# A layer with 32 streamed experts: another order of the output product, an earlier refill of its buffers, and a shorter chain to the first gathered tokens

## The chip, the cores and the metric

One core of a Trainium2 chip runs the whole program. The metric is the device time of one execution in microseconds (us), and the median of some runs of the same program counts.

## The reference

One layer over 256 tokens of width 1024, all float32. A mixer (short convolutions for one half of the channels, a gated linear recurrence for the other) is followed by an output product, a residual sum and a layer norm. Then each token chooses 4 of 32 experts, and the experts' outputs are mixed by their gates and normed again.

```python
mixed = _mixer(x, ...)                       # ends in einsum('bsc,cd->bsd', mix, w_out)
x = _layer_norm(DEEPNORM_ALPHA * x + mixed, ln1_g, ln1_b)
logits = x @ w_router + b_router
top_v, top_e = lax.top_k(logits, 4);  gates = softmax(top_v)
# for every expert e, for the tokens that chose it:
h = xb @ w_gu[e] + b_gu[e]                   # 1024 -> 2048
act = min(h_glu, 7) * sigmoid(1.702 * h_glu) * (clip(h_lin, -7, 7) + 1)
y = act @ w_dn[e] + b_dn[e]                  # 1024 -> 1024
x = _layer_norm(DEEPNORM_ALPHA * x + sum_of_gated_y, ln2_g, ln2_b)
```

The weights of one expert are 8 MB (gate and up) and 4 MB (down), so that the 32 experts make 403 MB of the 421 MB that the program moves.

## The kernel before

**Buffers.** `gu_buf` holds two experts' gate/up weights, 8 rows of 1 MB each (a row is 8 KB in each of 128 partitions); they are loaded in chunks of two rows, 2 MB (`load_gu`, `stream_gu`, lines 228 and 286). `dn_buf` holds one expert's down weights, 8 rows of 512 KB, loaded in halves of four rows, 2 MB (`load_dn`, `stream_dn_chunk`, lines 231 and 291). All loads are issued by the SP queue in the order in which its block is written out (lines 226 to 328). Each waits until the TensorE has used what stood in the place: `gu_used[c]`, `dn_used[c]`, or in the loading phase a named semaphore. While the mixer runs, second-set rows 2 to 5 of `gu_buf` hold the output weights `w_out_v` (8 rows of 512 KB, two in each row of `gu_buf`), and `dn_buf` holds scratch. Expert 1's first four down rows therefore go to free places elsewhere (`dn_extra`: the two rows of `late`, half of `mix`, half of `turned`; `load_extra`, line 261), and its last four into `dn_buf` once expert 0 has used them.

**The stretch around the change.** The output product (`mixer_out`, line 886) sums 8 blocks k for 4 tiles (two token halves h, two column halves c). Its first 4 blocks (the recurrence's) go for all tiles; then each tile in turn gets its last 4 blocks and is given to VectorE (`out_ps`). VectorE adds the residual, gathers statistics, centres and scales (`residual`, `centre`, `scale`; lines 599, 589, 593); TensorE transposes the un-normed sum (line 900) and multiplies by the router (`route_part`, 927; `route_sum`, 933). `choose` (632) takes the top four, TensorE counts ranks (945 to 949), and VectorE makes from them `places` (664), a token's slot in its expert. The first block of 32 token rows is gathered by `gather_first` in three sets of four products: first half with the finished values, second half with the bias `late[:,1]` and again with a scaled selector. VectorE transposes the rows (671), and `expert_block` starts: bias rows (999), 64 gate/up products (1005), the next block's gather (955), `combine`, and 64 down products (1038). Each product is recorded as two matmuls, so 1005 has 64 records for a block.

**Block 0 and after.** `expert_block(0, ..., first=True)` is unrolled. It is followed by a branch over a loop for further blocks of expert 0 (line 1057), and by `expert(1, ...)`, which loads two loop bounds (1047 and 1048) and loops over `expert_block`. The number of blocks up to each expert stands in `bounds`; VectorE writes it (685) after block 0's rows have been transposed. SP reads it for every expert (line 280) before it can wait for the right count. VectorE's own loop starts after the gates and the remaining `places` are known: it writes `gated` (717) and the next `onehot` (709), on which TensorE's next gather waits.

Of the kernel before, what the change touches and what calls it, by code (L numbers as in the profile page):

```python
# [27 lines left out]
P = 128  # L28
SLOTS = 32
# [13 lines left out]
def trunk(nc, x, w_in, conv_w, lru_conv_w, lru_conv_b, w_rgate, b_rgate, w_igate, b_igate, lru_lambda, w_out,  # L43
# [23 lines left out]
    with ExitStack() as ctx:  # L67
# [58 lines left out]
        hot_scaled = gated[:, 1, 0:SLOTS]  # L126
# [27 lines left out]
        quiet = rows_t[:, 0:P // SLOTS, :].rearrange("p k s -> p (k s)")  # L154
        ident_v = ident[:].rearrange("p (j e) -> p j e", j=GROUPS)
# [20 lines left out]
        def like(v, tile):  # L176
# [5 lines left out]
            "x_in0", "x_in1", "params_in", "matrices_in", "router_in", "wout_in0", "wout_in1", "ln1_in", "ln2_in", "bgu_in", "bdn_in", "extra_in", "stored",  # L182
# [5 lines left out]
            "mix_lru", "mix_conv", "lru_out_ps", "out_ps",  # L188

            "wsum_in", "wsum_ps", "wr_ok", "v_ok", "var_ok", "centred", "rstd_ok", "x1_ok", "vt_ps", "vt_sb", "lpart_ps", "lpart_sb", "logits_ps", "top_ok", "exp_in", "exp_ok",  # L190
# [35 lines left out]
        def _(sp):  # L226
# [41 lines left out]
            load_gu(1, 1, 1)  # L268
            sp.wait_ge(S["out_ps"], 2 * TH)
# [59 lines left out]
        def _(pool):  # L329
# [27 lines left out]
            nc.gpsimd.memset(closed, 0.0).then_inc(S["closed_zero"], 1)  # L357
            nc.gpsimd.memset(small[:, 380:382], -0.5).then_inc(S["consts"], 1)
# [3 lines left out]
            nc.gpsimd.memset(ones_row[:], 1.0).then_inc(S["ones_row"], 1)  # L362
# [14 lines left out]
        def _(act):  # L377
# [54 lines left out]
            for h in range(TH):  # L432
                for n in (2 * h, 2 * h + 1):
                    act.wait_ge(S["vt_ps"], n + 1)
                    nc.scalar.copy(x1t[:, h, CT * (n % 2):CT * (n % 2 + 1), :],
                                   ps[:, 4 + n, :].rearrange("p (k t) -> p k t", k=CT)).then_inc(S["vt_sb"], 1)
                act.wait_ge(S["lpart_ps"], h + 1)
                nc.scalar.copy(glu[:, P * h:P * (h + 1)], ps[:, HB + h, 0:P]).then_inc(S["lpart_sb"], 1)
            act.wait_ge(S["exp_in"], 1)
# [26 lines left out]
        def _(dve):  # L466
# [136 lines left out]
            def scale_0(c):  # L603
                dve.wait_ge(S["centred"], c + 1)
                dve.wait_ge(S["rstd_ok"], 1)
                dve.wait_ge(S["vt_ps"], c + 1)
                scale(0, c, mixed(0, c), xs[:, 0, 512 * c:512 * c + 512], late[:, 1, :], S["x1_ok"])

            def centre_in_place(c):
                dve.wait_ge(S["vt_ps"], 2 + c + 1)  # L610
                v = xs[:, 1, 512 * c:512 * c + 512]
                centre(1, c, v, v, late[:, 0, :], S["centred"])

            def scale_in_place(c):
                dve.wait_ge(S["centred"], 2 + c + 1)
                v = xs[:, 1, 512 * c:512 * c + 512]
                scale(1, c, v, v, late[:, 1, :], S["x1_ok"])
# [9 lines left out]
            total = small[:, 368:370]  # L627

# [17 lines left out]
            for c in range(2):  # L646
                centre(0, c, xs[:, 0, 512 * c:512 * c + 512], mixed(0, c), late[:, 0, :], S["centred"])
# [166 lines left out]
        def _(pe):  # L814
# [87 lines left out]
            for h in range(TH):  # L902
# [259 lines left out]
```

## Time and profile before

| | before |
|---|---|
| median of 3 runs | 1021.49 us (1020.88 to 1023.22) |
| the profiled execution | 1020.78 us |
| its span, first to last instruction | 1019.0 us |
| TensorE matmul / weight load | 824.2 us (81%) / 355.9 us (35%) |
| VectorE / ScalarE / GpSimd | 246.4 / 79.5 / 7.2 us |
| DMA | 421.69 MB, mean 414 GB/s |
| chain of waits, by engine | DMA 56%, PE 36%, DVE 5%, issue 2% |

The page cuts the span into 40 slices of 25.5 us. What to read first is the line of bytes moved per slice: it is level over nearly the whole span, and lower in the first five slices and the last.

### The profile page before, as it was taken

To read this page: it belongs to the slowest core of one execution; us is meant where nothing else is said; L and a number is where in the kernel's file an instruction comes from. 1 tells how busy PE (TensorE), PEld (TensorE's weight loads), DVE (VectorE), ACT (ScalarE), POOL (GpSimd) and SP (SyncE) were. 2 spreads that over 40 slices of the span, in tenths; PEclk is the share of its full clock that TensorE was granted. 3 is DMA by queue.
4 is the path that set the end of the run, shared out by engine and by line. 5 is a ranking of instruction groups with operands and counts; after the bars stand their busy time and mean duration, and the time that the engine had idled before them with its cause. 6 is when DMAs were issued, how large, how long until landed. Compare 5 with 4: busy or idle time off the path is not lost.

```text
span 1019.0 us, 20186 instructions
## 1 busy us (share of the span) xinstructions
PE 824.2 (81%) x8447; PEld 355.9 (35%) x8448; DVE 246.4 (24%) x692; ACT 79.5 (8%) x184; POOL 7.2 (1%) x25
## 2 busy tenths in 40 slices
PE   9999879898659999985699976666865885965995
PEld 7884433333213334331133421221321332311432
DVE  2473711221112222221112211111111221210233
ACT  1040100000000000000000000000000000000010
POOL 1000000000000000000000000000000000000000
PEclk9999989999899999998799998888989799988989
DMA  9988699999999999999999999999999999999996
GB/s 327 408 355 346 266 425 425 428 428 428 428 429 428 429 428 429 428 429 429 428 429 429 428 428 429 428 429 428 428 430 428 429 429 428 429 428 428 428 428 291
DMA packets 38903, 421.69 MB, mean 414 GB/s; under 512 B 5907, under 2 KB 6347, under 8 KB 14309
## 3 DMA queue, kind: packets, MB, share of 16 engines
q1 hardware_dynamic: 36436, 420.89, 98.0%
q10 hardware_dynamic: 2400, 0.44, 0.2%
q8 instruction: 14, 0.23, 0.1%
q0 software_dynamic: 48, 0.09, 0.0%
q14 instruction: 5, 0.03, 0.0%
HBM read 420.27 MB, written 1.18 MB: 414 GB/s over the span
## 4 chain that ended last, share of the span: by engine, by line
DMA 56%; PE 36%; DVE 5%; issue 2%; SPq 0%; DVEq 0%; POOLq 0%; ACT 0%; POOL 0%
DMA dn_buf<-in_w_down_dram 56%; PE ps L1038 12%; PE ps L1005 12%; PE ps L838 5%; PE ps L886 3%; PE ps L999 2%; PE ps L857 1%; DVE act_t L730 1%; DVE lin L725 1%; DVE lin L728 1%; DVE glu L722 1%; DVE lin L723 1%; DMA gu_buf<-in_w_in_dram 1%; PE ps L918 0%; PE ps L873 0%
## 5 line engine op out<-in xcount | busy, mean ns | idle before, releaser
L1005 PE MATMUL ps<-gu_buf,rows_t 128*32 128x512 f32 x2880 | 363.8, 651 | 102.0 <-DMA gu_buf<-in_w_gate_up_dram 102.0
L1005 PEld LDWEIGHTS ps<-gu_buf,rows_t 128*32 128x32 f32 x2880 | 93.8, 115 | 362.6 <-issue 196.0
L1038 PE MATMUL ps<-dn_buf,act_t 128*32 128x256 f32 x2848 | 171.1, 385 | 52.1 <-DMA dn_buf<-in_w_down_dram 44.1
L722 DVE TENSOR_SCALAR glu<-ps 128x256 f32<-128x256 f32 x45 | 19.1, 425 | 605.2 <-PE ps L1005 605.2
L1038 PEld LDWEIGHTS ps<-dn_buf,act_t 128*32 128x32 f32 x2848 | 87.7, 110 | 123.4 <-DMA dn_buf<-in_w_down_dram 59.2
L999 PE MATMUL ps<-turned,bias_sel 128*32 128x512 f32 x360 | 50.2, 630 | 22.6 <-issue 22.6
L449 ACT ACTIVATE sig<-glu 128x256 f32<-128x256 f32 x45 | 18.8, 417 | 529.1 <-DVE glu L722 529.1
L838 PE MATMUL ps<-turned,gu_buf 128*128 128x256 f32 x256 | 55.7, 379 | 0.0
L979 PE MATMUL ps<-mix,back 32*128 32x256 f32 x720 | 52.2, 404 | 0.5 <-ACT mix L453 0.5
L955 PE MATMUL ps<-xs,onehot 128*32 128x256 f32 x736 | 50.5, 394 | 1.5 <-DVE onehot L709 1.5
L838 PEld LDWEIGHTS ps<-turned,gu_buf 128*128 128x128 f32 x256 | 48.6, 190 | 6.9 <-issue 0.4
L979 PEld LDWEIGHTS ps<-mix,back 32*128 32x128 f32 x720 | 33.0, 187 | 21.0 <-issue 18.9
L955 PEld LDWEIGHTS ps<-xs,onehot 128*32 128x32 f32 x736 | 25.0, 115 | 40.8 <-issue 31.1
L717 DVE TENSOR_SCALAR gated<-onehot,gates 128x128 f32<-128x128 f32 x90 | 21.7, 284 | 70.2 <-issue 70.2
L453 ACT COPY mix<-ps 128x256 f32<-128x256 f32 x45 | 16.7, 372 | 209.3 <-PE ps L1038 209.3
L709 DVE TENSOR_SCALAR onehot<-slot_iota,block_base,places 128x128 f32<-128x128 f32 x92 | 27.8, 345 | 7.2 <-DVE gated L717 7.0
L730 DVE STREAM_TRANSPOSE act_t<-lin 128x256 f32<-128x256 f32 x45 | 28.9, 643 | 1.5
L886 PE MATMUL ps<-gu_buf,mix 128*128 128x512 f32 x64 | 28.0, 593 | 0.0
L999 PEld LDWEIGHTS ps<-turned,bias_sel 128*32 128x32 f32 x360 | 9.3, 112 | 39.4 <-issue 36.8
L451 ACT COPY back<-ps 128x256 f32<-128x256 f32 x45 | 16.8, 372 | 68.7 <-PE ps L973 68.7
L973 PE MATMUL ps<-ident,gated 128*128 128x128 f32 x90 | 19.6, 300 | 0.0
L728 DVE TENSOR_TENSOR lin<-lin,sig 128x256 f32<-128x256 f32 x45 | 19.1, 425 | 1.5
(234 smaller groups left out, 301.6 us busy)
## 6 DMA issues: line engine op xcount, KB each, us to landing
gu_buf<-in_w_gate_up_dram SPq DMA_DIRECT2D x128, 2048.0 KB, 30.2
dn_buf<-in_w_down_dram SPq DMA_DIRECT2D x62, 2048.0 KB, 13.3
gu_buf<-in_w_in_dram SPq DMA_DIRECT2D x4, 2048.0 KB, 18.4
gu_buf<-in_w_out_dram SPq DMA_DIRECT2D x2, 2048.0 KB, 16.9
dn_buf<-in_w_down_dram SPq DMA_DIRECT2D x2, 1024.0 KB, 27.1
xs<-in_x_dram SPq DMA_DIRECT2D x2, 512.0 KB, 5.4
gu_buf<-in_w_in_dram SPq DMA_DIRECT2D x2, 512.0 KB, 6.5
gu_buf<-in_w_in_dram SPq DMA_DIRECT2D x1, 1024.0 KB, 9.6
```

Of the source, the lines that this page charges most:

```text
L709: ins = V.tensor_scalar(onehot[:, h], slot_iota[:], base, column(h), ALU.add, ALU.is_equal)
L717: ins = V.tensor_scalar(gated[:, h, :], onehot[:, h].rearrange("p j s -> p (j s)"), gates[:, h, bass.ds(e, 1)], None, ALU.mult)
L722: V.tensor_scalar(glu[:], half(HB, 0), SWIGLU_LIMIT, None, ALU.min).then_inc(S["glu_ok"], 1)
L728: V.tensor_tensor(lin[:], lin[:], sig[:], ALU.mult).then_inc(S["act_ok"], 1)
L730: V.transpose(act_t[:], in_blocks(lin[:])).then_inc(S["act_t_sb"], 1)
L838: ins = T.matmul(half(banks[c // 2], c % 2), w_piece[:, piece_slot[i], k, P * c:P * (c + 1)], turned[:, k, :], start=(k == 0), stop=(k == ...
L886: return T.matmul(ps[:, 2 * h + c, :], mix[:, k, P * h:P * (h + 1)], w_out_v[:, n, 512 * c:512 * c + 512], start=(n == 0), stop=(n == KT - 1))
L955: ins = T.matmul(ps[SLOTS * j:SLOTS * (j + 1), Y0, 0:QF], onehot[:, h, 0, :], xs[:, h, QF * j:QF * (j + 1)], start=(h == 0), stop=(h == TH ...
L979: ins = T.matmul(ps[:, j, QF * h:QF * (h + 1)], stationary[SLOTS * j:SLOTS * (j + 1), P * h:P * (h + 1)], moving[SLOTS * j:SLOTS * (j + 1) ...
L999: T.matmul(ps[SLOTS * j:SLOTS * (j + 1), HB, :], bias_sel[:, j, :], b_gu, start=True, stop=False)
L1005: ins = T.matmul(ps[SLOTS * j:SLOTS * (j + 1), HB, :], rows_t[:, k, :], gu_buf[:, b, k, :].rearrange("p (two n) -> p two n", two=2)[:, :, ...
L1038: ins = T.matmul(ps[SLOTS * j:SLOTS * (j + 1), YB, 0:QF], act_t[:, DK * m + q, :], weights[q][:, QF * j:QF * (j + 1)], start=(m == 0 and q ...
```

## The change

**Output product.** Of the last four blocks, two go for all four tiles first (`wout_half` is raised), then the other two tile by tile. The row of `gu_buf` that held the first two blocks' weights is refilled on `wout_half` (1 MB, `gu_half`), the other on `out_ps` as before.

**Chain to the first gather.** The first half of the tokens is no longer scaled before the gather: `gather_first` has two sets of four products, each with a scaled selector (`hot_scaled[0]`, `hot_scaled[1]`), and the norm's bias is put into the sum ahead by products with a row of ones. The expert bias products of block 0 are issued ahead too, with a selector of their own. The router's second half is split in two, with `route_sum(0)` between. The idle products (`keep_warm`) go. On VectorE, the last centring is cut in two halves of 256 columns, the two full `onehot` writes and all four scalings (two per half) come after the gates.

**Refill.** The count of expert 0's blocks is written on its own (`first_ok`), before the first rows are transposed. SP then refills the first gate/up chunk in two parts, row 0 as soon as TensorE has used row 0 (`row_used`), row 1 with the chunk. Expert 1's down row 4 (`DK`) goes to four places of 128 KB (1 KB in each partition: `wr`, `turned`, `mix`, `mix`), loaded as soon as the router has used them; `dn_buf` then gets row 5 alone, and rows 6 and 7 together. Row 5 counts on the same semaphore as the quarters, `quarters_in`, and `expert(1, ...)` waits for all five at its head.

```diff
+            sp.wait_ge(S["wout_half"], 1)
+            sp.dma_start(gu_buf[:, 1, GK * 2, :], row_src[:, GK * 2, :]).then_inc(S["gu_half"], 16)
             sp.wait_ge(S["out_ps"], 2 * TH)
-            load_gu(1, 1, 2)
+            sp.dma_start(gu_buf[:, 1, GK * 2 + 1, :], row_src[:, GK * 2 + 1, :]).then_inc(gu_in[1][2], 16)
             sp.wait_ge(S["lpart_ps"], TH)
             load_extra(2)
             for j in range(GROUPS):
+                sp.dma_start(dn_quarters[j], dn_src[1][:, D * DK + QF * j:D * DK + QF * (j + 1)]).then_inc(S["quarters_in"], 16)
+            for j in range(GROUPS):
                 sp.dma_start(b_dn[E * j:E * (j + 1), :], b_down[0][:, QF * j:QF * (j + 1)]).then_inc(S["bdn_in"], 16)
-            sp.wait_ge(S["centred"], 2 * TH)
+            sp.wait_ge(S["centred"], 2 * TH + 1)
             load_extra(0)
-            sp.wait_ge(S["bounds_ok"], 1)
+            sp.wait_ge(S["first_ok"], 1)
...
-            stream_gu(2, 0, range(0, GC // 2))
+            used = blocks_before(1)
+            gu_row = gu_src[2].rearrange("p (k n) -> p k n", k=KT)
+            sp.wait_ge(S["row_used"], used)
+            sp.dma_start(gu_buf[:, 0, 0, :], gu_row[:, 0, :]).then_inc(S["row_in"], 16)
+            sp.wait_ge(gu_used[0], used)
+            sp.dma_start(gu_buf[:, 0, 1, :], gu_row[:, 1, :]).then_inc(gu_in[0][0], 16)
+            stream_gu(2, 0, range(1, GC // 2))
             sp.wait_ge(S["x1_ok"], 2 * TH)
             load_extra(1)
             stream_gu(2, 0, range(GC // 2, GC))
+            sp.wait_ge(S["bounds_ok"], 1)
             after_0 = blocks_before(1)
-            stream_dn_chunk(1, 1, after_0)
+            sp.wait_ge(dn_used[1], after_0)
+            sp.dma_start(dn_buf[:, DK + 1, :], dn_src[1][:, D * (DK + 1):D * (DK + 2)]).then_inc(S["quarters_in"], 16)
+            sp.dma_start(dn_buf[:, DK + 2:, :].rearrange("p q n -> p (q n)"), dn_src[1][:, D * (DK + 2):]).then_inc(dn_in[1], 16)
...
             link(choose(1))
             V.tensor_scalar(sel_bf, taken[:, :, 0:E], TAKEN, None, ALU.is_equal).then_inc(S["sel_ok"], 1)
-            V.tensor_scalar(sel, taken[:, :, 0:E], TAKEN, None, ALU.is_equal)
-            V.tensor_tensor(shifted, lg, top[:, :, 0:1].to_broadcast([P, TH, E]), ALU.subtract).then_inc(S["exp_in"], 1)
-            centre_in_place(1)
-            dve.wait_ge(S["exp_in"], 1)
-
+            link(V.tensor_scalar(sel, taken[:, :, 0:E], TAKEN, None, ALU.is_equal))
+            centre_half(1)
             dve.wait_ge(S["rank_ps"], 1)
             rank = ps[:, TB, 0:TH * E].rearrange("p (h e) -> p h e", h=TH)
             link(V.scalar_tensor_tensor(places[:], rank, 1.0, sel, ALU.add, ALU.mult))
-            V.tensor_scalar(hot_scaled, slot_count[:], places[:, 1, 0:1], small[:, 375:376], ALU.is_equal, ALU.mult)
             for h in range(TH):
-                ins = V.tensor_scalar(onehot[:, h], slot_iota[:], 1.0, places[:, h, 0:1], ALU.add, ALU.is_equal)
-            ins.then_inc(S["onehot0"], 1)
-            V.tensor_copy(bias_sel[:], ident_v[:, :, 0:1].to_broadcast([P, GROUPS, SLOTS])).then_inc(S["sel_bias"], 1)
+                V.tensor_scalar(hot_scaled[h], slot_count[:], places[:, h, 0:1], small[:, 374 + h:375 + h], ALU.is_equal, ALU.mult).then_inc(S["onehot0"], 1)
...
+            V.tensor_copy(bounds[0:1, 1:2], nb_i[0:1, 0:1]).then_inc(S["first_ok"], 1)
...
             V.tensor_tensor(gates[:], ex, total.unsqueeze(2).to_broadcast([P, TH, E]), ALU.mult).then_inc(S["gates_ok"], 1)
+            for h in range(TH):
+                V.tensor_scalar(onehot[:, h], slot_iota[:], 1.0, places[:, h, 0:1], ALU.add, ALU.is_equal)
+            for h in range(TH):
+                for c in range(2):
+                    scale_in_place(h, c)
             dve.wait_ge(S["closed_ps"], 1)
...
+            for n in range(CT // 2):
+                for h in range(TH):
+                    for c in range(2):
+                        ins = mixer_out(CT + n, h, c, n)
+            ins.then_inc(S["wout_half"], 1)
             for h in range(TH):
                 for c in range(2):
-                    for n in range(CT):
+                    for n in range(CT // 2, CT):
                         ins = mixer_out(CT + n, h, c, n)
                     ins.then_inc(S["out_ps"], 1)
...
-                pe.wait_ge(S["x1_ok"], 2)
-                for j in range(GROUPS):
-                    T.matmul(ps[SLOTS * j:SLOTS * (j + 1), Y0, 0:QF], onehot[:, 0, 0, :], xs[:, 0, QF * j:QF * (j + 1)], start=True, stop=False)
-                for j in range(GROUPS):
-                    T.matmul(ps[SLOTS * j:SLOTS * (j + 1), Y0, 0:QF], onehot[:, 1, 0, :], late[:, 1, QF * j:QF * (j + 1)], start=False, stop=False)
-                pe.wait_ge(S["centred"], 4)
-                for j in range(GROUPS):
-                    ins = T.matmul(ps[SLOTS * j:SLOTS * (j + 1), Y0, 0:QF], hot_scaled, xs[:, 1, QF * j:QF * (j + 1)], start=False, stop=True)
+                for h in range(TH):
+                    pe.wait_ge(S["onehot0"], h + 1)
+                    pe.wait_ge(S["centred"], 2 if h == 0 else 2 * TH + 1)
+                    for j in range(GROUPS):
+                        ins = T.matmul(ps[SLOTS * j:SLOTS * (j + 1), Y0, 0:QF], hot_scaled[h], xs[:, h, QF * j:QF * (j + 1)],
+                                       start=False, stop=(h == TH - 1), skip_group_check=True)
                 return ins
...
-            def expert(e, b, loads, down):
+            def expert(e, b, loads, down, also=None):
+                if also:
+                    pe.wait_ge(*also)
                 first = pe.value_load(bounds[0:1, bass.ds(e, 1)], min_val=1, max_val=MAXB - 1)
...
-            expert(1, 1, 16, [(S["extra_in"], 16 * GROUPS, dn_extra), down_at(1, 32)])
+            pe.wait_ge(S["gu_half"], 16)
+            expert(1, 1, 16, [(S["extra_in"], 16 * GROUPS, [quarters(v) for v in dn_extra]),
+                              (dn_in[1], 32, [dn_quarters] + down_at(1, 32)[2][1:])], (S["quarters_in"], 16 * (GROUPS + 1)))
```

## Rows read from the trace of the kernel before

**Rows 1.** The page: GB/s moved by the DMAs in 40 slices of 25.5 us.

```profile
GB/s 327 408 355 346 266 425 425 428 428 428 428 429 428 429 428 429 428 429 429 428 429 429 428 428 429 428 429 428 428 430 428 429 429 428 429 428 428 428 428 291
```

**Rows 2.** The chain of waits in order of time: start us, length us, what.

```profile
171.33 16.01 DMA dn_buf<-in_w_down_dram
```

**Rows 3.** Stretches: us, busy by engine, granted clock, DMA share, GB/s.

```profile
103.50:108.50 5.00, 5.00 (x34) 2.61 (x33) 3.59 (x6) 1.08 (x2) 0.00 (x0) 1.00 0.01 3
117.50:119.50 2.00, 2.00 (x21) 0.56 (x17) 1.96 (x7) 0.00 (x0) 0.00 (x0) 1.00 0.01 2
139.50:144.50 5.00, 4.85 (x24) 1.22 (x28) 0.00 (x0) 0.00 (x0) 0.00 (x0) 0.50 1.01 429
```

**Rows 4.** The SP queue in order of time: start us, us, line, DMA, count.

```profile
107.90 0.33 SPq L228 DMA_DIRECT2D gu_buf<-in_w_gate_up_dram  x1
110.89 0.33 SPq L261 DMA_DIRECT2D mix<-in_w_down_dram  x1
111.26 1.85 SPq L274 DMA_DIRECT2D mix<-in_b_down_dram  x4
113.72 0.35 SPq L261 DMA_DIRECT2D late<-in_w_down_dram  x1
118.74 2.44 SPq L286 DMA_DIRECT2D gu_buf<-in_w_gate_up_dram  x2
...
134.75 0.81 SPq L291 DMA_DIRECT2D dn_buf<-in_w_down_dram  x2
...
156.37 0.33 SPq L291 DMA_DIRECT2D dn_buf<-in_w_down_dram  x1
```

**Rows 5.** Issue to landing, for those issued at 107.9, 118.7, 134.75, 156.4, 201.7 us.

```profile
gu_buf<-in_w_gate_up_dram SPq DMA_DIRECT2D x1, 2048.0 KB, 7.2
gu_buf<-in_w_gate_up_dram SPq DMA_DIRECT2D x1, 2048.0 KB, 8.4
dn_buf<-in_w_down_dram SPq DMA_DIRECT2D x1, 2048.0 KB, 13.2
dn_buf<-in_w_down_dram SPq DMA_DIRECT2D x1, 2048.0 KB, 11.3
dn_buf<-in_w_down_dram SPq DMA_DIRECT2D x1, 2048.0 KB, 10.1
```

**Rows 6.** VectorE in order of time, with the idle time before and its releaser.

```profile
107.90 0.69 DVE L599 SCALAR_TENSOR_TENSOR xs<-xs,ps 128x512 f32<-128x512 f32 x1 [1.38 <-PE ps L886]
...
111.66 0.25 DVE L632 SCALAR_TENSOR_TENSOR small<-ps,small,b_rout 128x32 f32<-128x32 f32 x1 [0.42 <-PE ps L933]
...
113.61 0.22 DVE L664 SCALAR_TENSOR_TENSOR places<-ps,small 128x64 f32<-128x64 f32 x1
...
116.17 0.45 DVE L671 STREAM_TRANSPOSE rows_t<-ps 128x256 f32<-128x256 f32 x1 [1.49 <-PE ps L968]
...
117.98 1.41 DVE L593 SCALAR_TENSOR_TENSOR xs<-xs,small,late 128x512 f32<-128x512 f32 x2
...
124.85 0.48 DVE L717 TENSOR_SCALAR gated<-onehot,gates 128x128 f32<-128x128 f32 x2 [2.61 <-issue]
```

**Rows 7.** TensorE in order of time, with the idle time before and its releaser.

```profile
114.60 0.64 PE L963 MATMUL ps<-xs,onehot 128*32 128x256 f32 x8 [0.46 <-DVE onehot L667]
...
115.49 0.61 PE L968 MATMUL ps<-xs,gated 128*32 128x256 f32 x8
...
116.78 1.90 PE L1005 MATMUL ps<-gu_buf,rows_t 128*32 128x512 f32 x16
...
126.15 1.07 PE L955 MATMUL ps<-xs,onehot 128*32 128x256 f32 x16 [1.49 <-DVE onehot L709]
...
139.65 1.08 PE L999 MATMUL ps<-turned,bias_sel 128*32 128x512 f32 x4 [4.97 <-issue]
```

**Rows 8.** TensorE's queue, lines 1057 and 1047: duration ns min/median/max, first and last start.

```profile
L1057 PEldq COMPARE_BRANCH  x1: 3956/3956/3956, 134.1 to 134.1; - x1
L1047 PEldq TENSOR_LOAD <-bounds x30: 296/304/311, 138.1 to 966.7; - x30
```

More of the change, by code:

```diff
@@ L124, in trunk @@
         x1t = mix[:].rearrange("p k (h t) -> p h k t", h=TH)
-        hot_scaled = gated[:, 1, 0:SLOTS]
+        hot_scaled = [gated[:, 1, SLOTS * h:SLOTS * (h + 1)] for h in range(TH)]
+        first_sel = gated[:, 0, :].rearrange("p (j s) -> p j s", j=GROUPS)
         act_v = act_t[:].rearrange("p q s -> p (q s)")
@@ L627, in _ @@
             total = small[:, 368:370]
+            nb_i = small[:, 456:488].bitcast(I32)
             def choose(h):
@@ L645, in _ @@
             V.memset(lgx[:, :, E:], NO_LOGIT)
-            for c in range(2):
-                centre(0, c, xs[:, 0, 512 * c:512 * c + 512], mixed(0, c), late[:, 0, :], S["centred"])
+            dve.wait_ge(S["wsum_ps"], 1)
+            V.tensor_copy(first_sel, ident_v[:, :, 0:1].to_broadcast([P, GROUPS, SLOTS])).then_inc(S["sel_bias"], 1)
+            dve.wait_ge(S["ln1_in"], 32)
+            residual(0, 0)
+            link(residual(0, 1))
+            norm_variance(0, stats, S["var_ok"])
             residual(1, 0)
-            scale_0(0)
-            scale_0(1)
+            centre_in_place(0, 0)
+            centre_in_place(0, 1)
             link(residual(1, 1))
@@ L909, in _, with add_bias @@
                         turn_residual(0, 1)
-                    if h == 0 and c == 0:
-                        pe.wait_ge(S["wsum_in"], 1)
-                        T.matmul(ps[:, TB, 0:2 * E], gated[:, 0, :], small[:, 384:384 + 2 * E], start=True, stop=True).then_inc(S["wsum_ps"], 1)
+            def add_bias(now, picked):
+                pe.wait_ge(S["sel_bias"], now)
+                for j in range(GROUPS):
+                    T.matmul(ps[SLOTS * j:SLOTS * (j + 1), HB, :], picked[:, j, :], b_gu, start=True, stop=False)
             def start_sum():
@@ L935, in _ @@
             pe.wait_ge(S["wr_ok"], 1)
-            route_part(0)
+            pe.wait_ge(S["ones_row"], 1)
+            pe.wait_ge(S["ln1_in"], 32)
             turn_residual(1, 0)
+            route_part(0, range(GROUPS))
             turn_residual(1, 1)
+            route_part(1, range(GROUPS // 2))
             route_sum(0)
-            route_part(1)
+            route_part(1, range(GROUPS // 2, GROUPS))
             route_sum(1)
-            keep_warm(Y1, 6, ident[:])
+            pe.wait_ge(S["bgu_in"], 16 * GROUPS)
+            pe.wait_ge(S["lg_ok"], 1)
+            add_bias(1, first_sel)
+            pe.wait_ge(S["lg_ok"], TH)
+            for j in range(GROUPS):
+                T.matmul(ps[SLOTS * j:SLOTS * (j + 1), Y0, 0:QF], ones_row[:, 0:SLOTS], late[0:1, 1, QF * j:QF * (j + 1)], start=True, stop=False,
+                         skip_group_check=True)
             pe.wait_ge(S["sel_ok"], 1)
@@ L993, in turn_gates, with expert_block @@
                 ins.then_inc(S["gates_t_ps"], 1)
-            def expert_block(prior, now, b, loads, down, first=False):
-                pe.wait_ge(S["sel_bias"], now)
-                for j in range(GROUPS):
-                    T.matmul(ps[SLOTS * j:SLOTS * (j + 1), HB, :], bias_sel[:, j, :], b_gu, start=True, stop=False)
+            def expert_block(prior, now, b, loads, down, first=False, first_row=False):
+                if not first:
+                    add_bias(now, bias_sel)
                 pe.wait_ge(S["rows_t_ok"], now)
@@ L1082, in _ @@
             pe.wait_ge(S["ln2_in"], 32)
-            pe.wait_ge(S["ones_row"], 1)
             for n in range(2):
@@ L1097, in final_block @@
             def final_block(now, nth):
-                pe.wait_ge(S["sel_bias"], now)
-                for j in range(GROUPS):
-                    T.matmul(ps[SLOTS * j:SLOTS * (j + 1), HB, :], bias_sel[:, j, :], b_gu, start=True, stop=False)
+                add_bias(now, bias_sel)
                 pe.wait_ge(S["rows_t_ok"], now)
```

115 lines of the change are left out of this document (62 added, 53 removed).

## The prediction, made before the changed kernel ran

> **What bounds the kernel now.** I read the GB/s line of the page first [rows 1]: 428 or 429 in nearly every slice from the eighth on, 266 in the fifth, 291 in the last. A level line is a DMA that never rests, and the chain of waits says the same from 171.33 us on, where TensorE begins to wait for down weights and goes on doing so, expert after expert [rows 2]. So the end of the kernel is the time from which the stream of weights runs unbroken, plus bytes over 428 GB/s, plus a tail that the change doesn't touch. A microsecond in which the DMAs rest costs one; a microsecond of TensorE costs nothing unless it makes a refill late. I then looked, stretch by stretch, for the rests around the change. There are two: 103.5 to 108.5 us with 3 GB/s, where the last loads before the end of the output product are done and the next is issued at 107.90, and 117.5 to 119.5 with 2 GB/s, before the issue at 118.74 [rows 3, 4]. After that the stream is unbroken.
>
> The third view is how near to breaking it is later. A 2 MB load on idle DMAs lands 7.2 us after its issue, another that is soon joined by a second 8.4 [rows 5]. One that takes longer had others ahead of it, and the difference is the time by which it could have been issued later. The down loads of 134.75 took 13.2 us (6.0 of slack), that of 156.37 took 11.3 (4.1), that of 201.7 took 10.1 (2.9) [rows 5]. These slacks are what an earlier stream, or a later TensorE, uses up.
>
> **Part 1, earlier transfers in the first rest.** The last four blocks of the output product take 16 products, about 0.87 us each with their weights; the first eight are over near 100 us, so the 1 MB row goes out while the stream still has work, and fills 2.45 us (1 MB at 428 GB/s) of the first rest. That alone ends nothing sooner: what follows in the queue is again bound by TensorE and VectorE, and the rest just moves. What counts is the bytes moved before the final start of the stream, and when that start is. The bytes grow by the four quarters, 0.5 MB or 1.22 us. If pieces of 1 KB go at half the rate they occupy 2.4 us, but between 111.8 and 117 us there is room for it.
>
> SP issues more: four biases took 1.85 us [rows 4], so four quarters take as long. With `lpart_ps` at about 110.5 (110.89 now), SP gets to `load_extra(0)` at 114.4, not 113.72. Its cover is the wait for the first block, which lasts to 116.7; no cost.
>
> **Part 2, the chain to the first gather.** The tiles now end later but closer together: VectorE's 1.38 us of idle time before the last residual [rows 6] is used up, and that residual starts at about 108.1 instead of 107.90. Less work lies behind it (half a centring moved), and `route_part` in two pieces gives the second logits a little earlier. I put the second `choose` at 111.75 against 111.66 (bounds -0.4 and +0.5). From there `places` needs only the mask (0.2) and a half centring (0.35 to 0.4) instead of a full one, which brings it to 113.4 against 113.61 [rows 6]. From `places` to the transposes it was 2.56 us. Two full one-hot writes go (0.40), and one of three sets of products: the third started 0.89 after the first [rows 7], so 0.44 each. That leaves 1.72: transposes at 115.1 instead of 116.17 [rows 6], gate/up products at 115.6 instead of 116.78 [rows 7]. The bias products and idle products had no part in it after the change.
>
> SP now waits for the first row's eight records, not for the chunk: half of 1.90 [rows 7], so the issue is at 116.7 instead of 118.74. `first_ok` comes at about 114.7 and the register load behind it takes 1 us, in the cover of that wait. The start is 2.0 us earlier (bounds 1.5 and 2.5).
>
> **Gain at this point:** 1.22 + 2.04 = 3.3 us of stream (2.7 to 3.8).
>
> **Part 3, what moved behind the gates.** On VectorE two one-hot writes (0.4) and four scalings, two of which took 1.41 [rows 6], so 2.7 in all, now stand between the gates and the last `places`. Before, two scalings stood there (1.41), and the chain ahead was 1.1 later, plus two small operations that move ahead (0.4). Net: `places` 0.3 us later, and with it VectorE's first `gated` (124.85) and TensorE's gather, which already waited 1.49 us [rows 6, 7]: 126.5 instead of 126.15. SP's `load_extra(1)` is issued 0.5 us later with some 6 us of transfers queued ahead (two rows and a chunk, 9.8 us of data, begun at 118). Both hidden, the first by what comes next.
>
> **Part 4, the new wait.** `expert(1)` now waits at its head for `quarters_in` = 80, and the fifth part of that is down row 5, issued only when block 0 has used it: 135.0 us. It queues behind everything that SP issued before. The load in its place landed at 134.75 + 13.2 = 148.0. Row 5 needs only the first quarter of these bytes (1.5 MB or 3.7 us less) and the stream is 2.04 earlier: 142.3 us. The lower bound leaves out the 1.2 us by which a joined load landed later (8.4 against 7.2): 141.1. TensorE arrives at the wait when its branch of 3.96 us is done, at 138.1, or 138.4 now [rows 8]. So it stands for 3.9 us, and then still has the register loads ahead, 1.55 us (138.1 to 139.65). Expert 1 starts at 143.85 instead of 139.65 [rows 7]: 4.2 us late (3.0 to 4.7). Queued behind are all of expert 1, its `gu_used` and `dn_used`, and on these SP's next refills, issued at 145.06 and 156.37.
>
> The refill of 156.37 goes out at 160.6 and lands 7.2 to 8.4 later, 167.8 to 169.0. Before, it landed at 156.37 + 11.3 = 167.7. **The slack of 4.1 us is less than 3.3 + 4.2, and all of the gain is given back**: the stream rests for 3.2 to 3.4 us. The clock decides little: it was 0.50 in 139.5 to 144.5 after the idle 4.97 us [rows 3, 7]; a longer wait meets the same level on leaving it, and if it recovers a little sooner or later than the 5 us shown, that is -0.3 to +0.9 us on TensorE's lateness.
>
> The Trainium skill speaks against this place of the wait: "DMA: Bandwidth & Descriptors", section "Rules for kernel authors", has a DMA issued early and its semaphore waited for late. Row 5 is needed only by the down products, some 13 us after the head of the expert. By that rule, with the wait late, the sum would be that of rival A.
>
> **Afterwards.** Up to expert 3's first block TensorE is 4 us late, then it meets the down weights it waited for anyway and is 1 us late or less. The refill of 201.7 has 2.9 us of slack for that. Nothing more is lost.
>
> **Sum.** End = profiled time + (later landing of the refill of 156.37): 4.2 - 4.1 + (0 to 1.2) = +0.1 to +1.3 with my value of the wait; with its lower bound 3.0, -1.1 to +0.1. I take +0.2, as the stream will have rested just before, like the load of 7.2. 1020.78 + 0.2 = 1021.0. The runs' median lies 0.7 above the profiled execution, so the median should be 1021 to 1021.7: I say 1021.2. Its own range is 1019.7 to 1022.7.
>
> **Rivals.**
> A. *The wait isn't what I think*: row 5 lands before TensorE arrives, or refills are not what bounds 145 to 170 us. Then the 3.3 us come through: 1020.78 - 3.3 = 1017.5, as a median up to 1018.2. For it: the slacks before TensorE becomes the waiting side (6.0 and 4.1) both exceed 3.3, if TensorE isn't late. Against it: the order in SP's queue, and the landing time of the load in the same place. 0.24.
> B. *Slower*: expert 1 starts at the upper bound (4.7), the clock recovers a step later (+0.9), and the refill lands like a joined one (8.4): 4.7 + 0.9 - 4.1 + 1.2 = +2.7, so 1023.5. It is the same mechanism, TensorE's late refills in 143 to 168 us, and decides as slower once lateness and the joined landing together pass 6.1 us. For it: all loads after 118.74 land late by such a lag. 0.14.
> C. *The chain isn't shortened*: quarters and biases hold SP or the DMAs, or the compressed VectorE work makes the second logits late by 1 us. Then the stream starts 1 us earlier at most, row 5 lands later by as much, and expert 1 starts later: +1.2, 1022.2. 0.06.
> My forecast has 0.56.
>
> **Range and chances.** About 0.2%, 2.0 us, is what a measurement of this kernel can tell from no change. The range takes in the forecast, A and C and most of the way to B: 1017.6 to 1023.2. Faster 0.24 (A), same 0.58 (forecast and half of C), slower 0.18 (B, half of C, a rest).
>
> **What the profile will show.** Right: down loads in two parts at 135; a rest in the DMAs before 119 that ends near 118 instead of 120; the first gate/up products at 115.6; TensorE idle from 135 to nearly 144, with its first register load of line 1047's successor at about 142.4 instead of 138.1; rests of the DMAs between 148 and 162 adding up to the 3.3 us; and the level line from there on where it was. Wrong: expert 1 starting at 140, or a full stream from 120 to 170 with the end 3 us earlier.

## The result, and the profile after

| | before | after |
|---|---|---|
| median | 1022.30 us (20 runs, 1020.86 to 1024.42) | 1026.41 us (20 runs, 1023.09 to 1027.57) |
| the profiled execution | 1020.78 us | 1026.46 us |
| its span | 1019.0 us | 1024.7 us |

The changed kernel is slower: the ratio is 1.0034, with a 95% interval of 1.0027 to 1.0041, which is 3.5 us by the ratio and 4.1 by the medians. No change had been forecast, at 1021.2 us, and 1017.6 to 1023.2 us given as the range. The forecast stood on three runs of the kernel before with a median of 1021.49; in the 20 runs here it is 1022.30, so 0.8 us of the distance between 1021.2 and 1026.41 is not the change's.

The two profiled executions differ by 5.7 us, but not all of it is the change. In that of after, the first projection of the mixer, which the change doesn't touch, ran at the low clock (TensorE in order of time, start us, us):

```profile
7.29 5.34 PE L880 MATMUL ps<-turned,gu_buf 128*128 128x256 f32 x16
```

The same sixteen records took 3.69 us in the profile of before, and SP's issues from 65 us up to the output product are all 2.0 us later. Single executions differ in this. Below, times of different executions are therefore compared from one event, SP's issue of the last output row's refill: 107.90 us in before [rows 4], 109.91 in after. The new order of the output product stands ahead of it but doesn't move it: it comes 14.84 us behind SP's gate/up load of 93.06 us in before, and 14.83 behind the same load, at 95.08, in after. Times written as "+11.16" count from there.

The SP queue of after in order of time (start us, us, line, DMA):

```profile
109.91 0.33 SPq L276 DMA_DIRECT2D gu_buf<-in_w_gate_up_dram  x1
...
121.07 0.35 SPq L310 DMA_DIRECT2D gu_buf<-in_w_gate_up_dram  x1
...
138.46 0.33 SPq L320 DMA_DIRECT2D dn_buf<-in_w_down_dram  x1
...
165.65 0.33 SPq L299 DMA_DIRECT2D dn_buf<-in_w_down_dram  x1
```

The stream of weights starts for good at +11.16 (121.07), against +10.84 in before [rows 4]: 0.3 us later, not 2 us earlier. Down row 5 goes out at 138.46. The refill behind expert 1 goes out at +55.74; in before it was +48.47.

TensorE in order of time, with the idle time before and its releaser:

```profile
116.57 1.93 PE L1007 MATMUL ps<-xs,gated 128*32 128x256 f32 x16 [0.80 <-DVE gated L689]
119.07 3.64 PE L1041 MATMUL ps<-gu_buf,rows_t 128*32 128x512 f32 x16 [0.57 <-DVE rows_t L696]
...
129.87 1.07 PE L997 MATMUL ps<-xs,onehot 128*32 128x256 f32 x16 [0.95 <-DVE onehot L732]
...
149.13 1.94 PE L944 MATMUL ps<-turned,bias_sel 128*32 128x512 f32 x8 [10.74 <-issue]
```

Two things stand out. Block 0's first sixteen gate/up records take 3.64 us; in before they took 1.90 [rows 7]. And TensorE is idle for 10.74 us before expert 1, where it was 4.97 [rows 7]. The stretches that belong to them (us, busy by engine, granted clock, DMA share, GB/s):

```profile
117.00:123.00 6.00, 5.43 (x33) 1.16 (x25) 4.43 (x23) 0.26 (x1) 0.00 (x0) 0.50 0.61 181
144.00:149.00 5.00, 0.00 (x0) 0.00 (x0) 0.00 (x0) 0.00 (x0) 0.00 (x0) 0.50 1.01 418
```

In the first the granted clock is 0.50, the 1.2 GHz level, through the gather and the first gate/up rows. In the second TensorE has nothing to do while the DMAs are fully busy. What ended the idle time is in the chain of waits (start us, us, what):

```profile
138.46 9.04 DMA dn_buf<-in_w_down_dram
147.50 1.63 issue
149.13 1.94 PE ps L944 x8
```

The chain runs through down row 5, from its issue at 138.46 to its landing at 147.50, and the register loads behind it. In before the chain meets a down load only at 171.33 [rows 2].

VectorE in order of time:

```profile
112.42 0.25 DVE L656 SCALAR_TENSOR_TENSOR small<-ps,small,b_rout 128x32 f32<-128x32 f32 x1 [0.57 <-PE ps L966]
...
114.30 0.24 DVE L656 SCALAR_TENSOR_TENSOR small<-ps,small,b_rout 128x32 f32<-128x32 f32 x1
...
115.96 0.22 DVE L687 SCALAR_TENSOR_TENSOR places<-ps,small 128x64 f32<-128x64 f32 x1
...
118.57 0.45 DVE L696 STREAM_TRANSPOSE rows_t<-ps 128x256 f32<-128x256 f32 x1 [1.23 <-PE ps L1007]
```

`places` comes at +6.05 where it had been +5.71, and the transposes at +8.66 where they had been +8.27 [rows 6].

Last, the refill behind expert 1 (issued at 165.65) and row 5 (issued at 138.46), with us to landing:

```profile
dn_buf<-in_w_down_dram SPq DMA_DIRECT2D x1, 2048.0 KB, 8.6
dn_buf<-in_w_down_dram SPq DMA_DIRECT2D x1, 512.0 KB, 9.0
```

What this does to the DMAs (stretches as above):

```profile
150.00:165.00 15.00, 14.82 (x166) 5.64 (x162) 3.77 (x11) 0.79 (x2) 0.00 (x0) 0.87 0.88 355
166.00:171.00 5.00, 4.75 (x45) 1.52 (x49) 0.00 (x0) 0.03 (x1) 0.00 (x0) 1.00 0.89 333
```

Measured against 428 GB/s these are rests of 2.6 and 1.1 us, 3.7 together; in before the DMAs move 424 GB/s from 148 to 165 us. The whole loss can be read in this way. From the start of the span to +75 us, after moves 353 GB/s and before 366, which at 428 GB/s is 3.9 us of transfers less, and the execution ends 3.7 us later, counted from the common event.

### The profile page after: what moved, and what is told of

It reads as the page before. It is cut to its first block, busy times and chain, and to the rows that moved or that the text cites. A ratio compares the mean times of both kernels' runs of the same rounds, so it can differ in the third digit from the quotient of the medians.

```text
span 1024.7 us, 20159 instructions
## 1 busy us (share of the span) xinstructions
PE 830.1 (81%) x8427; PEld 356.0 (35%) x8428; DVE 246.8 (24%) x695; ACT 79.5 (8%) x184; POOL 7.2 (1%) x25
## 4 chain that ended last, share of the span: by engine, by line
DMA 56%; PE 36%; DVE 5%; issue 1%; DVEq 0%; SPq 0%; POOLq 0%; POOL 0%
DMA dn_buf<-in_w_down_dram 56%; PE ps L1076 12%; PE ps L1041 12%; PE ps L861 5%; PE ps L909 3%; PE ps L944 2%; PE ps L880 2%; DVE act_t L753 1%; DVE lin L751 1%; DVE lin L748 1%; DVE glu L745 1%; DVE lin L746 1%; DMA xs<-in_x_dram 0%; PE ps L950 0%; PE ps L852 0%
## 5 line engine op out<-in xcount | busy, mean ns | idle before, releaser
L1076 PEld LDWEIGHTS ps<-dn_buf,act_t 128*32 128x32 f32 x2840 | 87.5, 110 | 118.7 <-DMA dn_buf<-in_w_down_dram 54.4
L476 ACT COPY mix<-ps 128x256 f32<-128x256 f32 x45 | 16.7, 372 | 205.1 <-PE ps L1076 205.1
L474 ACT COPY back<-ps 128x256 f32<-128x256 f32 x45 | 16.7, 372 | 68.6 <-PE ps L1013 68.6
```

What stands on the lines that cost most here:

```text
L1076: ins = T.matmul(ps[SLOTS * j:SLOTS * (j + 1), YB, 0:QF], act_t[:, DK * m + q, :], weights[q][j], start=(m == 0 and q == 0), stop=(m == DC ...
```

## The experiments

Each was timed beside the kernel before, whose median was then 1022.7 to 1023.0 us (27 to 35 runs), against 1022.30 beside the changed kernel. Ratios are to the kernel before. Distances to the changed kernel are given as differences of medians; by the ratios they come out up to 0.5 us different (2.6 us for e1, 1.8 for e2, 3.6 for e3).

### The wait at the head of expert 1, moved: e1

```diff
             def expert(e, b, loads, down, also=None):
-                if also:
-                    pe.wait_ge(*also)
...
                 for m in range(DC):
                     landed, count, weights = down[m]
+                    if also and m == 1:
+                        pe.wait_ge(*also)
                     pe.wait_ge(landed, count)
```

> The changed kernel with one thing moved: TensorE's wait for the four quarters and down row 5 stands behind expert 1's gate/up products, just before the second half of its down products, and no longer at the head of expert 1. Theory 1 (the wait at the head makes TensorE and with it the refills late): in the changed kernel's trace the branch is done at 144.2 us and the wait ends at 147.5, so expert 1 starts 3.3 us earlier (145.8 instead of 149.1), the down load that follows it is issued and lands 3.3 us earlier, and the end is 3 to 4 us earlier, about 1023. Rival (the later start of the stream of weights, not the wait, sets the end): expert 1 starts earlier, the DMAs just rest less in 150 to 166 us, and the time stays within 1 us of the changed kernel's 1026.4.

Measured: 1023.74 us (12 runs), ratio 1.0009 [1.0000, 1.0017]; 2.7 us below the changed kernel. TensorE, and two stretches:

```profile
114.35 1.07 PE L1007 MATMUL ps<-xs,gated 128*32 128x256 f32 x16 [0.80 <-DVE gated L689]
...
143.86 1.93 PE L944 MATMUL ps<-turned,bias_sel 128*32 128x512 f32 x8 [6.90 <-issue]
```

```profile
114.30:118.00 3.70, 3.08 (x33) 0.97 (x33) 3.06 (x18) 0.26 (x1) 0.00 (x0) 1.00 0.86 253
127.20:130.50 3.30, 3.30 (x18) 2.02 (x10) 2.13 (x6) 0.31 (x1) 0.00 (x0) 0.50 0.99 413
```

The idle time before expert 1 is 6.90 us instead of 10.74, expert 1 starts at +36.2 instead of +39.2, and 2.7 of the 4.1 us of loss are gone (3 to 4 were expected). The wait is a cause. The second thing here is that in this execution the clock was 1.00 through the first gather, which took 1.07 us for the records that took 1.93 above, with the same order of work up to there. The fall in the changed kernel isn't bound to the order alone. The second stretch lies behind the next gather, before which TensorE was idle for 2.89 us; e3 takes this up.

### The idle products, put back: e2, and both edits: e3

```diff
+            keep_warm(Y1, 2, ident[:])
             pe.wait_ge(S["sel_ok"], 1)
...
+            keep_warm(Y1, 3, ident[:])
             gather_first().then_inc(S["rows0_ps"], 1)
+            keep_warm(Y1, 2, ident[:])
```

> The changed kernel with idle 128x128 products put back: 2 before the wait for the selection, 3 before the first gather, 2 behind it. Their results are not used. Theory 1 (without them the granted clock fell to 0.50 from 116.4 to 123.3 us, through the gather and the first rows of block 0): the clock stays at 1.00 there, the first row's refill goes out 1.5 to 2 us earlier after the start, row 5 lands 2 to 3 us earlier and so does the end: about 1024. Rival (the clock's fall there is chance, its step lands differently in each execution): no change in the median, 1026.4.

> Both edits, the late wait and the idle products. If both causes are real and add up: 3.3 + 2 to 2.5 us below the changed kernel, 1020.5 to 1021.5, so 1 us or so below the kernel before (1022.3). If the gain of the earlier stream (3.3 us by the prediction's sum) comes through in full: 1019. If only one of them counts, it is the same as the better of the two single edits.

Measured: e2 1024.20 us (10 runs), 1.0016 [1.0003, 1.0029], 2.2 us below the changed kernel. e3 1022.36 (12 runs), 0.9999 [0.9988, 1.0009]: the two edits together bring 4.0 us, which is about all of the loss, but nothing of the gain that the change was to bring; 1020.5 to 1021.5 had been expected. Part of why not is in e3's profile. (Its execution took 1025.4 us, the slowest of e3's; the clock fell at the same place, behind 2.89 and 2.88 us of idle time, in the profiles of e1 and e2.) TensorE, then VectorE:

```profile
129.04 1.07 PE L998 MATMUL ps<-xs,onehot 128*32 128x256 f32 x16 [2.90 <-DVE onehot L732]
130.04 5.36 PE L950 MATMUL ps<-xs,scaled_ident 128*128 128x256 f32 x16
```

```profile
127.74 0.48 DVE L740 TENSOR_SCALAR gated<-onehot,gates 128x128 f32<-128x128 f32 x2 [2.62 <-issue]
```

TensorE now waits 2.90 us for the one-hot of the next gather, 1.49 in before [rows 7], and the clock falls behind it: the start of the sum takes 5.36 us, against 3.72 at the full clock in after. The down products of block 0 begin at +25.8, in before at +23.1. At +11 the DMAs are 1.5 us of transfers ahead of before; at +75 they are 0.6 behind. This is a candidate for a third cause, which isn't in the prediction: I had called the late one-hot hidden. Behind +75 this execution lost another 2.2 us, and why stays open.

### The wait alone, in the kernel before: e4

```diff
             def expert(e, b, loads, down):
+                if isinstance(e, int) and e == 1:
+                    pe.wait_ge(dn_in[1], 32)
                 first = pe.value_load(bounds[0:1, bass.ds(e, 1)], min_val=1, max_val=MAXB - 1)
```

> The kernel before with one wait added: TensorE waits at the head of expert 1 for the second half of its down weights, which it needed only in the down products. In the trace of before they land at 148.0 us. Theory 1: expert 1 starts at 148.0 + 1.55 = 149.5 instead of 139.65, the down load of 156.4 is issued at 166.2 and lands at 173.4 instead of 167.7, and the end is 5 to 7 us later: about 1028. Rival (TensorE's lateness is taken up by the queue of transfers): under 1.5 us.

Measured: 1028.78 us (5 runs), 1.0062 [1.0049, 1.0075], or 6 us. TensorE before expert 1, and the refill behind it:

```profile
149.91 1.94 PE L999 MATMUL ps<-turned,bias_sel 128*32 128x512 f32 x8 [15.27 <-issue]
```

```profile
dn_buf<-in_w_down_dram SPq DMA_DIRECT2D x1, 2048.0 KB, 8.4
```

Expert 1 starts at 149.91 (expected 149.5), the refill goes out at 166.26 (166.2) and lands 8.4 us later. This is the cleanest proof of the mechanism: one wait of nothing new, on data that were in time anyway. The refill goes out 9.9 us late (+58.4 against +48.5); less the 4.1 us of slack, plus 1.2 for the joined landing, that is 7.0 us. The profiled execution ended 6.6 us later from the common event, the medians differ by 5.8.

### The late one-hot: e5 and e6

e5 moves the four scalings; e6 leaves them and fills TensorE's idle time. Both start from e3.

```diff
             link(V.scalar_tensor_tensor(places[:], places[:], -1.0, sel, ALU.add, ALU.add))
+            for h in range(TH):
+                for c in range(2):
+                    scale_in_place(h, c)      # e5; taken away ahead of closed_ps
...
+                if first:
+                    keep_warm(Y0, 10, ident[:])      # e6
                 pe.wait_ge(S["onehot_ok"], now)
```

> The kernel of e3 (late wait, idle products) with VectorE's four scalings moved from behind the gates to behind the last places, where VectorE's queue stands 2.6 us in register loads before its loop. In e3 TensorE waited 2.90 us for the next one-hot, and its clock then fell to 0.50 for 3.4 us. Theory 3 (the moved scalings make the gather late, and the clock with it): the gather starts 2.7 us earlier after the start, TensorE idles under 0.5 us there, the clock stays at 1.00, the down products start 2.5 to 4 us earlier, the down load behind expert 1 likewise until its slack is there, and the end is 2 us earlier than e3's 1022.4: about 1020.4. Rival (the register loads wait until VectorE has done all work, or the lateness is taken up by the queue): the gather stays where it is, 1022.4.

> The kernel of e3 with 10 idle 128x128 products (2.2 us) while TensorE waits 2.9 us for the one-hot before block 0's gather. Theory 3, the part of the clock alone: the clock stays at 1.00 from 127 to 131 us (after the start of e1), the down products start 1.6 us earlier than in e3, and the end is 1 to 1.5 us earlier, 1021. Rival: no clock fall there in most executions, no change, 1022.4.

Measured: e5 1020.41 us (12 runs), 0.9976 [0.9968, 0.9985]; e6 1020.62 (12 runs), 0.9981 [0.9970, 0.9993]. Both are faster than the kernel before. e5's VectorE and TensorE:

```profile
122.32 2.74 DVE L616 SCALAR_TENSOR_TENSOR xs<-xs,small,late 128x512 f32<-128x512 f32 x4
124.98 0.47 DVE L740 TENSOR_SCALAR gated<-onehot,gates 128x128 f32<-128x128 f32 x2
```

```profile
126.27 1.07 PE L998 MATMUL ps<-xs,onehot 128*32 128x256 f32 x16 [0.30 <-DVE onehot L732]
```

The four scalings take 2.74 us, and the loop's first instruction follows on them with no gap: the register loads, which had stood as 2.62 us of "issue", run beside them. (This execution took 1024.8 us as a whole, the slowest of e5's, so only its rows up to +75 are read.) TensorE waits 0.30 us, and its gather starts at +16.7, in e3 at +19.3. e6's gather and its stretch:

```profile
127.29 1.07 PE L998 MATMUL ps<-xs,onehot 128*32 128x256 f32 x16 [0.45 <-DVE onehot L732]
```

```profile
126.00:131.00 5.00, 4.55 (x37) 3.46 (x36) 3.67 (x11) 0.42 (x1) 0.00 (x0) 1.00 0.99 416
```

Here the gather is as late as in e3 (+19.2) and the clock stays up: the down products start at +24.1, 1.7 us earlier than in e3. But expert 1 starts 3.8 us earlier (+31.7), and 2.1 of these are another thing: TensorE's branch behind block 0 took 2.90 us here and 5.01 in e3 (see "The branch" below). The medians differ by 1.7 us. So e6 doesn't separate what the clock is worth from the shorter branch. In e5 the branch took 4.71 us, close to e3's, so that its 2.0 us against e3 are mostly the earlier gather and the clock, which e5 changes together. Both kernels keep what the DMAs are ahead: at +75 it is 1.9 us (e5) and 1.8 (e6); what e5's execution lost came behind that.

### The idle products in the kernel before: e7, and the changed kernel again: e8

```diff
-            keep_warm(Y1, 6, ident[:])
...
-            keep_warm(Y1, 4, ident[:])
```

> The kernel before without its idle products (6 before the ranks, 4 before the first gather); nothing else. Theory 2 (idle products keep the granted clock up through the first gather): the clock falls to 0.50 near 116 us in at least some executions, block 0's first chunk takes up to 1.8 us longer and the stream of weights starts up to 2 us later, so the median is 1 to 2 us over the kernel before. Rival (in the kernel before there is other work enough): within 0.5 us.

> The changed kernel once more, for another look. In its first profile the clock fell at 116.4 us, in that of e1, with the same order of work up to there, it did not. If the fall is a matter of the moment (the other theory of e2), it will be at another place or absent; if it is the order of work alone, it is at 116 again. The branch of TensorE behind block 0 took 3.96 us before and 6.41 after; here it is measured again.

Measured: e7 1023.80 us (11 runs), 1.0008 [0.9999, 1.0017]: 0.9 us, inside its noise and between theory and rival. Its profile shows the fall:

```profile
116.08 1.08 PE L962 MATMUL ps<-xs,onehot 128*32 128x256 f32 x8 [1.46 <-DVE onehot L667]
```

```profile
115.60:118.80 3.20, 2.72 (x28) 1.34 (x32) 0.56 (x4) 0.00 (x0) 0.00 (x0) 0.50 0.95 365
```

Eight records of the gather took 0.64 us in before [rows 7] and 1.08 here, and the stream of weights starts at +12.2 instead of +10.8. In e8, the changed kernel once more (one run, 1026.05 us), the clock is low at the same place; its branch took 6.46 us:

```profile
116.00:122.00 6.00, 5.43 (x32) 1.17 (x32) 4.39 (x24) 0.26 (x1) 0.00 (x0) 0.50 0.62 182
```

Over all profiles: of the five executions of kernels without idle products, four had the low clock at the first gather, and e1 had not; of the nine with them none had. So the products matter, and chance does too. The four whose clock fell had also run the mixer's first projection at the low clock (4.93 to 5.37 us), and e1 had not (3.69); with idle products five of nine ran it slowly (4.50 to 5.39) and kept the clock at the gather all the same. What sets this apart from one execution to the next isn't shown. The median moved by 0.9 us in the kernel before and by 2.2 in the changed one. In e7 only the gather and the bias products were slow, and the first sixteen gate/up records took 1.89 us; in the changed kernel these were slow as well.

### Parts of the change alone: e9, e10, e11, and one more order: e12

e9 is the kernel before with the four quarters and the split of the last down rows, and the wait late as in e1. e10 is the kernel before with the output product's new order and `wout_half` alone. e11 is the changed kernel with only e5's move of the scalings. e12 is e5 with this:

```diff
-            sp.wait_ge(S["x1_ok"], 2 * TH)
-            load_extra(1)
             stream_gu(2, 0, range(GC // 2, GC))
+            sp.wait_ge(S["x1_ok"], 2 * TH)
+            load_extra(1)
```

> The kernel before with the four quarters and the split of expert 1's last down rows alone, and TensorE's wait for them late, before the second half of the down products. 0.5 MB more is moved before the stream's second rest ends. Theory (bytes moved in the rests count one for one while the down load behind expert 1 has 4.1 us of slack): 1.2 us below the kernel before, 1021.7. Rival (the quarters hold up the SP queue or the load behind them): 0 or above.

> The kernel before with the new order of the output product and the 1 MB row refilled on its half, nothing else. The prediction had: fills 2.45 us of the first rest, and ends nothing sooner, since the stream's final start is set by the chain to block 0. In the kernel before the second rest (117.5 to 119.9 us) then begins earlier and is longer. Expected: within 0.5 us of the kernel before. Rival (every byte moved in the first rest counts): 2.4 us below. A cost: the last residual 0.1 to 0.3 us later.

> The changed kernel with only the four scalings moved behind the last places (the edit of e5), the wait at the head of expert 1 and the missing idle products as they are. Theory 1 (TensorE stands at the wait for row 5, which lands late): the gather and down products start 2 to 3 us earlier, but expert 1 only as much as row 5 lands earlier, which is under 1 us; the end moves by under 1 us from 1026.4. Rival (the late gather is a cause of its own): 2 us or more below.

> The kernel of e5 with SP's load of the second extra row (which waits for the last scaling) put behind the two chunks that follow it. In e5 the first of these went out at 126.0 us, held by that wait until 125.1, where its chunk had been used by about 123.7. Theory: the stream has no rest there in either, so it brings 0 to 0.5 us against e5's 1020.4. Rival (the held chunk makes a rest): 1 us or more below e5.

| | median, us | ratio to before |
|---|---|---|
| e9, quarters alone | 1021.24 (12 runs) | 0.9983 [0.9972, 0.9994] |
| e10, product order alone | 1024.05 (12 runs) | 1.0010 [1.0000, 1.0019] |
| e11, changed, scalings moved | 1025.16 (12 runs) | 1.0020 [1.0007, 1.0034] |
| e12, e5 with extra row later | 1021.11 (12 runs) | 0.9983 [0.9970, 0.9997] |

The quarters bring 1.5 us where 1.2 were expected: bytes moved in a rest count one for one, as long as the refill behind expert 1 has slack (its landing took 10.5 us in e9, so 3.3 us were left). Its profile ends 0.9 us earlier from the common event. The new product order alone costs 1.3 us, where no more than 0.5 was expected (the interval just reaches no change), and VectorE shows why:

```profile
111.46 0.68 DVE L602 SCALAR_TENSOR_TENSOR xs<-xs,ps 128x512 f32<-128x512 f32 x1
```

SP's issue on the last tile was at 109.48 there, so this last residual starts at +1.98; in before it started with it, after 1.38 us of idle time [rows 6]. With all tiles ending close together, VectorE's two scalings of the first half stand before it. The changed kernel doesn't have them there, and its last residual is at +0.10. The stream of weights starts at +12.6 in e10, in before at +10.8. e11 brings 1.2 us against the changed kernel, between theory and rival; with an interval of 0.0013 on either side it rules out neither. Its profile is on the side of the theory: row 5 went out 1.2 us earlier than in after (+27.4) but took 11.3 us, and expert 1 started no earlier (+40.4). e12 isn't told apart from e5.

## Why the prediction was wrong

**What held.** The stream of weights bounds the kernel, and a rest of the DMAs costs what it lasts: e9. The wait for row 5 at the head of expert 1 stops TensorE, which makes the refill behind expert 1 late, and only lateness above its 4.1 us of slack counts: e4 and e1. The sum's last line can be done again with the measured values. The refill was issued 55.74 - 48.47 = 7.3 us late and landed 8.6 us after its issue, not 11.3: 7.3 - 4.1 + (8.6 - 7.2) = 4.6 us. That it landed so much later (+64.3, in before +59.8) is the same numbers over again; what tests the sum is the end, 3.7 us later in the profile and 4.1 in the medians. The bytes that are missing at +75 us, taken at 428 GB/s, foretell the end in most profiles: 6.5 us behind and 6.6 later at the end in e4, 1.0 ahead and 0.9 earlier in e9. In nine of the thirteen profiles beside before's the two agree within 0.6 us; e2, e3 and e5 end 1.7 to 4.2 us later than that, and why isn't known. This is rival B's mechanism, with a lateness of 7.3 where B had 4.7 and 0.9 for the clock. With the joined landing it is past the 6.1 us that I had given as the point of decision. The rests of 3.7 us come near the 3.2 to 3.4 that I had named, but in part by luck: my terms were 3.3 + 4.2 - 4.1, and the measured ones are 0.9 (the quarters' 1.2 less the stream's later start of 0.3), 7.3 and 4.1.

**The step that failed** is in part 2: "The bias products and idle products had no part in it after the change." I took the idle products away without asking what they hid, and forecast the gather and the first gate/up rows at their durations of before. The clock fell there in the profiles of after, e8 and e11, and sixteen records of the gather and of the gate/up products took 1.93 and 3.64 us, where e1 with the clock up took 1.07 and 1.93. The terms, from the common event:

| | forecast | after | e3 (clock up) |
|---|---|---|---|
| first gate/up product | +7.7 | +9.2 | +8.5 |
| issue of the stream's first row | +8.8 | +11.2 | +9.6 |
| landing of row 5 | +34.4 | +37.6 | +36.1 |
| expert 1 starts | +36.0 | +39.2 | +35.5 (wait late) |

Of the 2.4 us by which the first row's issue was missed, 1.6 to 1.7 go with the clock (the issue is at +9.6 in e3 and at +9.4 in e1, which has no idle products). The rest is the chain of VectorE: the first `choose` waited 0.57 us for `route_sum(0)`, which starts at +2.1 and not at +1.4 as in before, since a transposition now runs ahead of `route_part(0)` and half of the second `route_part` ahead of the sum; the second `choose` followed at +4.4, not +3.85. So with the clock up the stream starts 1.3 to 1.4 us earlier than in before: 0.4 to 0.6 by the shorter chain, for which I had 1.2, and the rest by the issue behind one row instead of two. Without the clock both are lost, and it starts 0.3 us later.

This went on into part 4. I had expert 1 4.2 us late, and it was 7.5: row 5 was issued at +28.55 where I had +27.1, which is 1.4 us, and took 9.04 us to land where I had 7.3, because I had counted the stream as 2 us earlier. The last term that was too small is the landing of the refill behind expert 1: 8.6 us, where I took 7.4 out of 7.2 to 8.4. Together with the 0.8 us of the kernel before this is about the whole distance from 1021.2 to 1026.41.

**A second miss**, in part 3: the later gather was put at 0.3 us and called hidden. With the clock up (e3) it is 1.0 us: I had the chain ahead 1.1 us earlier, and it was 0.3 (transposes at +7.95 in e3, at +8.27 in before). Behind the idle time of 2.9 us before it the clock falls again, 1.6 us more. e5 takes both away and gains 2.0 us; e6 takes away the fall, with a shorter branch beside it. In the changed kernel itself it hardly shows (idle time 0.95, since TensorE was slow before it).

**The branch.** TensorE's branch over expert 0's loop took 3.96 us in before [rows 8]. In after:

```profile
L1099 PEldq COMPARE_BRANCH  x1: 6406/6406/6406, 137.8 to 137.8; - x1
L1089 PEldq TENSOR_LOAD <-bounds x30: 297/303/312, 147.6 to 973.3; - x30
```

It ends at 144.2 while row 5 lands at 147.5, so the wait covers it here. In e1 it is bare, 5.86 us, and accounts for 1.9 of the 4.4 us by which expert 1 is still late there. Its length over all profiles was 2.90 to 6.68 us (the last section has them by group). What sets it stays open; no run varied it alone, and it differs between kernels that I compare: it took 6.68 us in e7 and 3.96 in before. That cost little there: e7's refill behind expert 1 still took 9.2 us to land, with 2.0 of slack left, and its execution ended 1.5 us later, close to the 1.4 by which its stream started later. For e6 it can't be set aside.

**Rivals.** A, the whole gain, came nearest in e5, e6 and e12, at 1020.4 to 1021.1 us: 1.6 to 2.5 us below the kernel before, where the sum had 3.3. C, the chain not shortened, is what the clock made true in the changed kernel, though for another reason than I gave.

The range failed too. It took its upper end from bounds on each term but left out the event that two of them rested on, that the clock stays up.

The rule that I had weighed, of the Trainium skill's "DMA: Bandwidth & Descriptors", section "Rules for kernel authors", to issue early and wait late, agrees with e1 and e4: the same wait, early or late, differs by 2.7 us in the changed kernel and 6 us in the kernel before. Its use here, that with the wait late the sum would be rival A's, did not hold: e1 is 0.8 us above the kernel before.

## What to carry to other kernels

When a change takes idle-looking work from TensorE or lengthens a wait of it, ask what the clock does next, and add the durations behind it at both levels of the clock. In a kernel that a stream of loads bounds, find the refill with the least slack and add up lateness there; put a wait for a load where its data are used, not at the head of the block. And put VectorE's work that nobody waits for yet in front of register loads, where its queue stands anyway. When an experiment changes one thing, read its whole profile against the other's: here the length of a branch changed along with it.

## What the runs showed of the hardware

The register loads ahead of VectorE's loop ran beside four operations issued before them: 2.62 us of "issue" (e3) became none (e5).

The branch over expert 0's loop on TensorE's queue took from 2.90 to 6.68 us in fourteen profiles, at the same place of the work, with the DMAs fully busy. In the five kernels without idle products it took 5.86 to 6.68 us, in the nine with them 2.90 to 5.01. The clock at the gather doesn't explain it, since e1 had it up and took 5.86. Where the branch and its target lie in the program may, but that wasn't tried.

TensorE's records before the fall in the changed kernel look busy: between 113.4 and 116.4 us they cover 2.2 of 3 us, with idle times of 0.20 us and, up to the gather at 116.57, 0.80. What filled them was mostly products of 32 columns or of a single row. The kernels that had a few 128x128 products there kept the clock. What of this decides was not tried.
